# A hybrid decoder step on one core: other orders on GpSimd, VectorE and ScalarE, and a plain fp32 last product

## The chip, the core and the metric

The kernel runs on one core of one Trainium2 chip. The metric is device microseconds (us) of one execution, the median of several runs. A profiled execution gives the trace; its span is the time from the first to the last instruction, a little less than the execution's own time. TensorE is called PE, its weight loads PEld, VectorE DVE, ScalarE ACT, GpSimd POOL and SyncE SP, as in the profile.

## What is computed

One layer of a decoder trunk for 512 prompt tokens and 64 sample tokens (8 sequences of 8), width 1024, all in fp32:

```python
def layer(x, ...):                       # prompt and sample group alike
    h = rmsnorm(x, norm1_g)
    a, b, q, k, v, g = split(h @ w_in)   # 2 x 512 conv columns, 4 x 512 retention columns
    c = silu(layernorm(causal_depthwise_conv(a * sigmoid(b))))        # 31 taps
    o, new_state = retention(rope(q), rope(k), v, state)              # 4 heads, decay per head
    o = silu(g) * groupnorm(o)
    x = x + concat(c, o) @ w_out
    x = x + hier_moe(rmsnorm(x, norm2_g))      # 4 groups x 8 experts, top 2 experts of the top group
    x = x + rmsnorm(p @ w_ple) * sigmoid(x @ w_ple_gate)
    return x, new_conv_buffer, new_state
# hier_moe: hid = silu(t @ w_gate[e]) * (t @ w_up[e]);  y += gate * (hid @ w_down[e]),  32 experts, 256 wide
```

A last RMSNorm ends it. The conv buffers and the retention states of both groups are outputs too.

## The kernel before

The 576 tokens lie in five tiles: 0 to 3 are the prompt's 128 rows each, 4 the 64 sample rows. Each engine has its own program, written out by hand, and they meet at named semaphores: what an engine does next is the order of its own program, and a wait holds up all that stands behind it there.

**Products in three parts.** Most products are made in fp32r, with each operand split in a high part (a rounded copy, mostly by ACT) and a low part (operand less high part, by DVE or POOL). PE adds three products: high by high, then high weight by low operand (`which` 1 in the output projection), then low weight (`which` 2). So a weight chunk `c` needs `w_high(c)` on ACT (L1462) and `w_low(c)` on POOL (L1791) or DVE. A few products are plain fp32 and need no parts: the router, the embedding product with `ple_weights`, and the retention.

**Output projection.** `w_out_part(c, i)` makes chunk `c` (12 to 15, 256 columns each) of tile `i`: 24 matmuls. The order on PE is (12,0), `gated_T(3)`, (12,1) to (12,3), `retention_out(4)`, (13,0) to (13,3), `gated_T(4)`, `sample_states` for heads 0 and 1, (12,4), (13,4), `sample_states` for heads 2 and 3, `p_T`, and then (14,i) and (15,i) by tile with `p_T`, the router and the transposes `h2_T` between them. The first of them waits for `z_sb` 40, ACT's last copy of the input projection (`z_out(11,4)`).

**What feeds it.** `heads_high(i)` (ACT, L1535) and `heads_low(i)` (DVE, L1076) split the retention half of tile `i`; `add_x(c,i)` (DVE, L1071) adds a chunk to the residual. For each tile DVE makes `qTx` (L1091, L1096 for the sample tile), `Sm` (L1103), the group norm's statistics (L1131 to L1136), and, after POOL's power (`grs`, L1859), the normalised output (L1139); POOL then gates it (L1866), which `gated_T(i)` waits for. POOL also makes the key decay (`kz`, L1835), the masked sample queries (`qmask`, L1852, from `qTx`) and value masks for even heads (`v_masks`, L1842); DVE makes those for odd heads (L1082). DVE's L1153 adds to the sample states, which an ACT-queue transfer (`rs_out`) then stores.

**First router norm.** `x1_sq(i)` (ACT, L1584 and L1587) makes the sum of squares and the root, `norm2(i)` (DVE, L1171 and L1176) the normalised tile, `h2_T(i)` on PE the transpose. `norm2(0)` waits for `rs_out`, since it writes where the states lie. `pT_out(n, ...)` (ACT, L1612) copies the transposes that `p_T` makes.

**Experts.** 32 experts, each one step: PE does `gate_up` (48 matmuls), the next expert's `x_T`, the former expert's `down` and `hid_T`. ACT copies high parts (`x_out` L1658, `w_high_part` L1607, `hid_high` L1682, `down_high` L1689) and the result (`y_copy` L1677); DVE makes low parts (`x_low` L1296, `w_low` L1165, `hid_low` L1310, `down_low` L1317). POOL gathers token rows and scatters results. Weights come in a ring of six 1 MB slots, loaded by SP as they are freed. After the last scatter the results are read back and the embedding gate follows.

Of the kernel before, what the change touches and what calls it, by code (L numbers as in the profile page):

```python
# [28 lines left out]
P = 128  # L29
# [95 lines left out]
def build(nc, ins, outs):  # L125
# [8 lines left out]
    with ExitStack() as ctx:  # L134
# [272 lines left out]
        def _(sp):  # L407
# [75 lines left out]
            with sp.If(n_ov > 0):  # L483
                sp.wait_ge(S["d_done"], NE)
# [16 lines left out]
        def _(pe):  # L501
# [356 lines left out]

            def down(i, q):
# [37 lines left out]
            down(LOOPS - 1, NX - 1)  # L897
# [63 lines left out]
        def _(dve):  # L961
# [123 lines left out]
            for i in range(TT):  # L1085
# [8 lines left out]
                else:  # L1094
                    for h in range(NH):
                        m = V.tensor_tensor(qTx[:, h, 0:NS].rearrange("p (b t) -> p b t", b=NB),  # L1096
                                            qTs[:, h, 0:NS].rearrange("p (b t) -> p b t", b=NB),
                                            bc(C("xi")[:, h * P:h * P + NL], 1, NB), ALU.mult)
                        if h == NH - 1:
                            m.then_inc(S["qTx_sb"], 1)  # L1100
# [16 lines left out]
                if i == TT - 1:  # L1117
                    for t in range(TT - 1):
                        heads_low(t)
                    for t in range(TT - 1):  # L1120
                        add_x(12, t)
# [14 lines left out]
                V.tensor_scalar(mv[0:r, :, 1], mv[0:r, :, 1], EPS, None, ALU.add).then_inc(S["gn_var"], 1)  # L1136
                dve.wait_ge(S["gn_rstd"], i + 1)
# [6 lines left out]
            for n in range(2 * NH):  # L1144
                h, a = n // 2, n % 2
                if n == 4:
                    heads_low(TT - 1)
                    add_x(12, TT - 1)
                    add_x(13, TT - 1)
                    v_masks(3)  # L1150
# [169 lines left out]
            def step(i, q, first=False, last=False):  # L1320
# [6 lines left out]
                hid_low(i, q)  # L1327
                down_low(i, q)

            w_low(0, 0, 1)  # L1330
            x_low(0, 0)
# [113 lines left out]
        def _(act):  # L1445
# [126 lines left out]
            heads_high(TT - 1)  # L1572
            w_high(14)
# [80 lines left out]
            def x_out(i, q):  # L1654
                i, par = 2 * i + q // 2, q % 2
                act.wait_ge(S["xt_ps"], 2 * i + par + 1)
                for a in range(2):
# [8 lines left out]
            def y_copy(i, q):  # L1666
                i, par = 2 * i + q // 2, q % 2
                act.wait_ge(S["d_done"], 2 * i + par + 1)
# [7 lines left out]
                for a in range(2):  # L1676
                    A.activation(yout[:, par, a * 512:(a + 1) * 512], bank[5 + a][:, :], ACT.Copy).then_inc(S["y_ready"], 1)  # L1677

# [12 lines left out]
            def step(i, q, first=False, last=False):  # L1691
# [7 lines left out]
                hid_high(i, q)  # L1699
# [287 lines left out]
```

## Time and profile before

| | us |
|---|---|
| runs | 782.49, 783.19, 784.65 (median 783.19) |
| the profiled execution, its own time | 783.66 |
| its span | 781.6 |
| PE busy | 705.3 |
| DVE busy | 556.6 |
| ACT busy | 398.2 |
| POOL busy | 325.9 |

What lies outside the span is 2.06 us. In timeline rows the first number is the start from the span's begin, the second the time taken, and a bracket at the end tells how long the engine had been idle and what ended that. PEclk is the clock granted to TensorE as a share of 2.4 GHz: 1.00 is 2.4 GHz, 0.50 is 1.2 GHz, and a value between is a stretch with both.

### The profile page before, as it was taken

The page shows a single profiled execution, that of the slowest core. Times are in us where ns is not written, and L with a number is a line of the kernel's source. Part 1 is how long each engine was busy: PE and PEld are TensorE (multiplying, and loading weights), DVE is VectorE, ACT ScalarE, POOL GpSimd, SP SyncE. Part 2 cuts the span into 40 slices and gives each one's busy share as a digit, 9 for nine tenths or more (in the row PEclk, how much of TensorE's full clock was granted, in tenths as well). Part 3 has the DMA queues.
Part 4 walks back from the last instruction along what each step waited for, and adds up shares of the span by engine and source line. Part 5 has one row for each costly group of instructions (what it writes and reads, how often), then busy time and mean ns, then how long its engine had stood idle before and what let it go on. Part 6 is the DMA issues. An engine that isn't in the chain of part 4 may idle for free.

```text
span 781.6 us, 13739 instructions
## 1 busy us (share of the span) xinstructions
PE 705.3 (90%) x5152; PEld 657.4 (84%) x5152; DVE 556.6 (71%) x801; ACT 398.2 (51%) x514; POOL 325.9 (42%) x230
## 2 busy tenths in 40 slices
PE   2979999999988987996899999999999999937995
PEld 1879999998978857963888999999999999827994
DVE  4579999804664262355798888888888888847653
ACT  4321332235440022154678888888888888642221
POOL 3222479971455130002256666666666664110000
PEclk9899999999998988999899999999999999977998
DMA  9631331130037234170588999999999999566211
GB/s 283 196 90 55 109 102 62 55 108 11 2 122 245 68 121 149 56 282 15 180 306 321 344 337 340 348 348 366 380 380 375 366 363 359 206 207 212 60 50 41
DMA packets 54301, 156.67 MB, mean 200 GB/s; under 512 B 8825, under 2 KB 34617, under 8 KB 41129
## 3 DMA queue, kind: packets, MB, share of 16 engines
q1 hardware_dynamic: 38516, 134.03, 47.6%
q10 hardware_dynamic: 9597, 12.58, 5.2%
q0 software_dynamic: 6144, 9.45, 3.5%
q8 instruction: 30, 0.49, 0.2%
q14 instruction: 14, 0.11, 0.0%
HBM read 150.34 MB, written 17.59 MB: 215 GB/s over the span
## 4 chain that ended last, share of the span: by engine, by line
PE 71%; DVE 10%; issue 6%; ACT 4%; DMA 4%; POOL 3%; ACTq 1%; POOLq 0%; DVEq 0%
PE bank L503 65%; PE bank L507 6%; DVE ring_parts L1165 3%; DMA ring<-in_w_expert_up 1%; POOL ring_parts L1791 1%; ACT down_high L1689 1%; DMA gbc<-in_norm_g 1%; DVE hT_high L1296 1%; DVE scratch L986 1%; DVE qTx L1096 1%; DVE z L1139 1%; ACT front L1677 1%; POOL z L1866 1%; DMA uext<-expert_rows 1%; DVE ring_parts L1317 1%
## 5 line engine op out<-in xcount | busy, mean ns | idle before, releaser
L503 PE MATMUL bank<-ring_parts,hT_high 128*128 128x256 f32 (+1 forms) x1552 | 216.8, 285 | 0.0
L503 PEld LDWEIGHTS bank<-ring_parts,hT_high 128*128 128x128 f32 (+1 forms) x1552 | 198.5, 186 | 0.1
L503 PE MATMUL bank<-catT_parts,hT_high 128*128 128x256 f32 x1064 | 148.8, 287 | 5.8 <-DVE hT_high L1296 3.3
L1165 DVE TENSOR_TENSOR ring_parts<-ring,catT_parts 128x2048 fp32r<-128x2048 f32 x64 | 146.4, 2288 | 5.0 <-ACT catT_parts L1607 4.9
L503 PEld LDWEIGHTS bank<-catT_parts,hT_high 128*128 128x128 f32 x1064 | 134.3, 191 | 8.2 <-DVE hT_high L1296 4.6
L1607 ACT ACTIVATE catT_parts<-ring 128x2048 fp32r<-128x2048 f32 x64 | 122.6, 1915 | 22.2 <-PE bank L503 19.1
L1791 POOL TENSOR_TENSOR ring_parts<-ring,ring_parts 128x2048 fp32r<-128x2048 f32 x15 | 69.0, 4602 | 69.5 <-ACT ring_parts L1462 69.1
L1317 DVE TENSOR_TENSOR ring_parts<-ring,down_high 128x2048 fp32r<-128x2048 f32 x32 | 73.4, 2293 | 29.4 <-ACT down_high L1689 29.4
L1043 DVE SCALAR_TENSOR_TENSOR bank<-uext,cpar,bank 128x512 f32<-128x512 f32 x116 | 87.9, 757 | 0.0
L1913 POOL DMA_INDIRECT expert_rows<-front,cur_code x32 | 33.9, 1059 | 96.5 <-issue 88.1
L503 PE MATMUL bank<-down_high,cv_parts 128*128 128x512 f32 x256 | 68.9, 412 | 3.1 <-ACT down_high L1689 3.1
L1689 ACT ACTIVATE down_high<-ring 128x2048 fp32r<-128x2048 f32 x32 | 61.7, 1927 | 0.0
L1506 ACT ACTIVATE z<-bank 128x256 f32<-128x256 f32 (+1 forms) x40 | 15.4, 384 | 82.3 <-PE bank L503 82.3
L503 PEld LDWEIGHTS bank<-down_high,cv_parts 128*128 128x128 f32 x256 | 46.6, 192 | 12.2 <-issue 3.2
L1882 POOL COPY cur_tok<-tokidx 128x1 int32 (+1 forms) x28 | 52.6, 1880 | 0.0
L1677 ACT ACTIVATE front<-bank 128x512 f32<-128x512 f32 x64 | 34.8, 596 | 33.1 <-PE bank L503 33.1
L1882 POOL COPY cur_code<-codes 128x1 int32 (+1 forms) x32 | 47.9, 1497 | 0.2
L1462 ACT ACTIVATE ring_parts<-ring 128x2048 fp32r<-128x2048 f32 x15 | 28.6, 1907 | 35.6 <-PE bank L503 35.6
L1296 DVE TENSOR_TENSOR hT_high<-bank,hT_high 128x512 fp32r<-128x512 f32 x64 | 40.9, 679 | 6.6 <-ACT hT_high L1658 6.6
L507 PE MATMUL bank<-const,scratch 128*128 128x128 f32 (+1 forms) x176 | 26.7, 302 | 20.6 <-DVE scratch L986 15.4
L503 PE MATMUL bank<-hT_high,ring_parts 128*128 128x256 f32 (+1 forms) x256 | 39.7, 307 | 5.4 <-ACT catT L1500 4.1
L503 PE MATMUL bank<-ring_parts,hT_low 128*128 128x256 f32 (+1 forms) x320 | 44.5, 282 | 0.0
(250 smaller groups left out, 1113.2 us busy)
## 6 DMA issues: line engine op xcount, KB each, us to landing
ring<-in_w_expert_gate SPq DMA_DIRECT2D x32, 1024.0 KB
ring<-in_w_expert_up SPq DMA_DIRECT2D x32, 1024.0 KB
ring<-in_w_expert_down SPq DMA_DIRECT2D x32, 1024.0 KB, 7.3
ring<-in_w_in SPq DMA_DIRECT2D x12, 1024.0 KB, 5.3
ring<-in_w_out SPq DMA_DIRECT2D x4, 1024.0 KB, 4.9
ring<-in_w_ple_gate SPq DMA_DIRECT2D x4, 1024.0 KB, 6.5
catT<-in_x_prompt SPq DMA_DIRECT2D x4, 512.0 KB, 8.2
z<-in_x_prompt SPq DMA_DIRECT2D x4, 512.0 KB, 6.0
```

The lines of the kernel that those rows point to most:

```text
L503: return nc.tensor.matmul(out, lhsT, rhs, start=start, stop=stop, skip_group_check=True)
L507: return nc.tensor.transpose(out, in_, ident[0:k, 0:k])
L1043: V.scalar_tensor_tensor(out, uext[:, c, t:t + SEQ], tap, bank[7][:, :], ALU.mult, ALU.add).then_inc(S["convp"], 1)
L1165: V.tensor_tensor(ring_r[:, 3 * par + m, :], ring[:, 3 * par + m, :], cat_r[:, m * CHUNK:(m + 1) * CHUNK].bitcast(F32), ALU.subtract).then ...
L1296: m = V.tensor_tensor(XT_lo[:, par, 4 * a:4 * a + 4, :], bank[2 + a][:, :].rearrange("p (k s) -> p k s", k=4), XT_hi[:, par, 4 * a:4 * a + ...
L1317: V.tensor_tensor(ring_r[:, 3 * par + 2, :], ring[:, 3 * par + 2, :], down_hi[:, :].bitcast(F32), ALU.subtract).then_inc(S["dn_lo"], 1)
L1607: A.activation(cat_r[:, m * CHUNK:(m + 1) * CHUNK], ring[:, s, :], ACT.Copy).then_inc(S["w_hi"], 1)
L1677: A.activation(yout[:, par, a * 512:(a + 1) * 512], bank[5 + a][:, :], ACT.Copy).then_inc(S["y_ready"], 1)
L1689: A.activation(down_hi[:, :], ring[:, 3 * par + 2, :], ACT.Copy).then_inc(S["dn_hi"], 1)
L1791: G.tensor_tensor(ring_r[:, c % 4, :], ring[:, c % 4, :], ring_r[:, 4 + c % 2, :].bitcast(F32), ALU.subtract).then_inc(S["w_lo"], 1)
L1882: G.tensor_copy(dst, src[:, bass.ds(n, 1)]).then_inc(done, 1)
L1913: G.indirect_dma_start(moe_d, bass.IndirectOffsetOnAxis(ap=cur_code[0:r, par:par + 1], axis=0), yout[0:r, par, :], None, bounds_check=2 * ...
```

## The change

In the tile loop of the retention, GpSimd's `w_low(12)` comes ahead of its wait for the statistics of tile 3 and no longer behind the power; ACT's `heads_high(0)` comes ahead of `z_out(11,4)`, `heads_high(1)` ahead of `w_high(13)`; DVE's `heads_low(0)` comes into tile 3, ahead of the wait for the power; the sample tile's `qTx` is one instruction for the four heads. DVE's `v_masks(3)` comes ahead of two `add_x`. ACT gets a dummy root ahead of `w_high(14)` and a dummy silu ahead of the first expert; the third `pT_out` goes behind the first router sum of squares; the second half of the first expert's `x_out` goes to DVE. The last expert's down product is plain fp32: four products in place of twelve, without the parts of the weights and of the hidden rows, its two halves signalled and copied apart. The signal count that SP waits for in the overflow branch rises by one with it.

```diff
@@ PE, last expert (NE = 32)
+            def down_plain(i, q):
+                i, par = 2 * i + q // 2, q % 2
+                pe.wait_ge(S["hT_ev"], 2 * (2 * i + par) + 1)
+                pe.wait_ge(slot_in[3 * par + 2], 16 * i + 16 * (LOADS[3 * par + 2] + 1))
+                pe.wait_ge(S["y_ready"], 2 * (2 * i + par))
+                for a in range(2):
+                    for k in range(2):
+                        m = mm(bank[5 + a][:, :], hidT[:, par, k, :], slot2(3 * par + 2)[:, k, a * 512:(a + 1) * 512],
+                               k == 0, k == 1)
+                    m.then_inc(S["d_done"], 1)
-            down(LOOPS - 1, NX - 1)
+            down_plain(LOOPS - 1, NX - 1)
@@ DVE, tile loop
-                    for h in range(NH):
-                        m = V.tensor_tensor(qTx[:, h, 0:NS].rearrange("p (b t) -> p b t", b=NB),
...
+                    V.tensor_tensor(qTx[:, :, 0:NS].rearrange("p h (b t) -> p h b t", b=NB),
+                                    qTs[:, :, 0:NS].rearrange("p h (b t) -> p h b t", b=NB),
+                                    bc(C("xi").rearrange("p (h t) -> p h t", h=NH)[:, :, 0:NL], 2, NB),
+                                    ALU.mult).then_inc(S["qTx_sb"], 1)
...
-                    for t in range(TT - 1):
+                    for t in range(1, TT - 1):
                         heads_low(t)
...
                 V.tensor_scalar(mv[0:r, :, 1], mv[0:r, :, 1], EPS, None, ALU.add).then_inc(S["gn_var"], 1)
+                if i == TT - 2:
+                    heads_low(0)
                 dve.wait_ge(S["gn_rstd"], i + 1)
@@ DVE, sample states
                     heads_low(TT - 1)
+                    v_masks(3)
                     add_x(12, TT - 1)
                     add_x(13, TT - 1)
-                    v_masks(3)
@@ DVE, experts
-                hid_low(i, q)
-                down_low(i, q)
+                    hid_low(i, q)
+                    down_low(i, q)
             w_low(0, 0, 1)
+            dve.wait_ge(S["xt_ps"], 1)
+            V.tensor_copy(XT_hi[:, 0, 4:8, :], bank[3][:, :].rearrange("p (k s) -> p k s", k=4)).then_inc(S["xt_sb"], 1)
             x_low(0, 0)
@@ ACT, tile loop
+                if i == TT - 1:
+                    heads_high(0)
                 z_out(11, i)
...
                 if i == TT - 1:
-                    heads_high(0)
+                    heads_high(1)
                     w_high(13)
-                    heads_high(1)
                     heads_high(2)
...
             heads_high(TT - 1)
+            A.activation(rst4[:, 0:1], epsb[:, :], ACT.Sqrt)
             w_high(14)
@@ ACT, first router norm
-            pT_out(3, (4,))
             for i in range(TT):
+                if i == 1:
+                    pT_out(3, (4,))
                 if i >= 2:
                     h2_out_low(i - 2)
@@ ACT, experts
+            A.activation(rst4[:, 0:1], epsb[:, :], ACT.Silu)
-            x_out(0, 0)
+            x_out(0, 0, first=True)                 # the first half only
...
+                if last:
+                    hid_plain(i, q)                 # one plain copy of the hidden rows
+                else:
+                    hid_high(i, q)
+                    down_high(i, q)
...
-            y_copy(LOOPS - 1, NX - 1)
+            y_copy(LOOPS - 1, NX - 1, last=True)    # waits for each half by itself
@@ POOL, tile loop
+                if i == TT - 2:
+                    w_low(12)
                 pool.wait_ge(S["gn_var"], i + 1)
                 G.tensor_tensor(grs[0:r, :], mv[0:r, :, 1], half[0:r, 0:NH], ALU.pow).then_inc(S["gn_rstd"], 1)
-                if i == TT - 2:
-                    w_low(12)
```

## Rows read from the trace of the kernel before

**Rows 1.** Busy time by stretch: PE, PEld, DVE, ACT, POOL; PEclk, DMA share, GB/s.

```profile
259.00:271.00 12.00, 12.00 (x100) 11.70 (x100) 3.95 (x16) 0.00 (x0) 2.28 (x2) 1.00 0.35 111
293.00:294.00 1.00, 1.00 (x8) 1.00 (x8) 0.26 (x1) 0.00 (x0) 0.00 (x0) 0.64 0.98 226
313.00:315.00 2.00, 2.00 (x14) 2.00 (x14) 0.35 (x1) 0.00 (x0) 0.00 (x0) 0.70 0.40 160
361.00:363.60 2.60, 2.54 (x18) 0.86 (x15) 1.72 (x7) 1.17 (x4) 0.00 (x0) 1.00 0.00 0
433.00:643.00 210.00, 210.00 (x1527) 198.32 (x1526) 186.34 (x153) 177.26 (x196) 131.90 (x87) 1.00 0.97 358
689.40:691.00 1.60, 1.56 (x4) 1.30 (x5) 1.60 (x1) 0.00 (x0) 0.05 (x1) 0.58 1.10 377
```

**Rows 2.** The timeline from 222 to 251 us, all engines.

```profile
222.67 1.90 ACT L1462 ACTIVATE ring_parts<-ring 128x2048 fp32r<-128x2048 f32 x1
...
228.43 4.55 POOL L1791 TENSOR_TENSOR ring_parts<-ring,ring_parts 128x2048 fp32r<-128x2048 f32 x1
...
229.31 0.62 ACT L1535 ACTIVATE hT_high<-catT 128x512 fp32r<-128x512 f32 x1
...
229.60 0.76 SPq L432 DMA_DIRECT2D front<-in_state_ret  x1
...
229.77 5.78 DVE L1096 TENSOR_TENSOR qTx<-qTs,const 128x64 f32<-128x64 f32 x4
...
233.94 1.26 POOL L1866 TENSOR_TENSOR z<-z 128x512 f32<-128x512 f32 x1
...
235.81 1.88 DVE L1076 TENSOR_TENSOR catT_parts<-catT,hT_high 128x512 fp32r<-128x512 f32 x3
...
236.53 2.07 PE L503 MATMUL bank<-ring_parts,catT_parts 128*128 128x256 f32 x8 [5.28 <-DVE catT_parts L1076]
...
240.11 1.06 PE L507 MATMUL bank<-const,z 128*128 128x128 f32 x4
...
250.30 1.96 PE L503 MATMUL bank<-front,uext 128*64 128x128 f32 x16
...
250.48 0.42 DVE L1071 TENSOR_TENSOR z<-bank,z 128x256 f32<-128x256 f32 x1 [1.51 <-PE bank L503]
```

**Rows 3.** The timeline: one mask alone at 209 us, then 280 to 292 us.

```profile
209.88 1.72 DVE L1082 TENSOR_TENSOR cv<-z,const 64x1024 f32<-64x1024 f32 x1
...
280.39 4.52 POOL L1791 TENSOR_TENSOR ring_parts<-ring,ring_parts 128x2048 fp32r<-128x2048 f32 x1 [5.29 <-ACT ring_parts L1462]
...
281.48 4.51 DVE L1082 TENSOR_TENSOR cv<-z,const 64x1024 f32<-64x1024 f32 x1
...
286.73 3.60 PE L503 MATMUL bank<-cv,kz 64*128 64x512 f32 x4 [3.72 <-DVE front L1153]
...
291.05 1.20 PE L503 MATMUL bank<-ring_parts,conv_high 128*128 128x256 f32 x4
```

**Rows 4.** The timeline at the first router norm.

```profile
304.94 1.05 ACT L1584 ACTIVATE front<-z 128x1024 f32<-128x1024 f32 x1
...
309.26 1.97 PE L507 MATMUL bank<-const,front 128*128 128x128 f32 x8 [4.53 <-DVE front L1176]
```

**Rows 5.** DMA issues: engine queue, count, KB, median us from issue to landing.

```profile
out<-front ACTq DMA_DIRECT2D x1, 2048.0 KB, 10.2
front<-in_state_ret SPq DMA_DIRECT2D x1, 0.5 KB, 13.2
```

**Rows 6.** The timeline: a plain fp32 product, a short gap at 360, the last expert.

```profile
337.42 3.60 PE L503 MATMUL bank<-ple_weights,uext 128*128 128x512 f32 x8
...
360.83 0.84 PE L503 MATMUL bank<-one_hots 128*128 128x80 bf16 x10 [1.32 <-DVE one_hots L1267]
...
689.44 3.56 PE L503 MATMUL bank<-down_high,cv_parts 128*128 128x512 f32 x8 [3.06 <-ACT down_high L1689]
694.06 1.09 ACT L1677 ACTIVATE front<-bank 128x512 f32<-128x512 f32 x2 [4.72 <-PE bank L503]
```

More of the change, by code:

```diff
@@ L483, in _ @@
             with sp.If(n_ov > 0):
-                sp.wait_ge(S["d_done"], NE)
+                sp.wait_ge(S["d_done"], NE + 1)
                 with sp.Fori(0, NOV) as j:
@@ L1094, in _ @@
                 else:
-                    for h in range(NH):
-                        m = V.tensor_tensor(qTx[:, h, 0:NS].rearrange("p (b t) -> p b t", b=NB),
[L1097 to L1100, printed above, removed]
+                    V.tensor_tensor(qTx[:, :, 0:NS].rearrange("p h (b t) -> p h b t", b=NB),
+                                    qTs[:, :, 0:NS].rearrange("p h (b t) -> p h b t", b=NB),
+                                    bc(C("xi").rearrange("p (h t) -> p h t", h=NH)[:, :, 0:NL], 2, NB),
+                                    ALU.mult).then_inc(S["qTx_sb"], 1)
                     decay = C("decay_s", NS).rearrange("p (h t) -> p h t", h=NH)
@@ L1652, in xt_half, with x_out @@
                 return XT[:, par, 0:4, :], bank[2][:, :].rearrange("p (k s) -> p k s", k=4)
-            def x_out(i, q):
+            def x_out(i, q, first=False):
                 i, par = 2 * i + q // 2, q % 2
                 act.wait_ge(S["xt_ps"], 2 * i + par + 1)
-                for a in range(2):
+                for a in range(1 if first else 2):
                     A.activation(XT_hi[:, par, 4 * a:4 * a + 4, :], bank[2 + a][:, :].rearrange("p (k s) -> p k s", k=4),
@@ L1664, in silu, with y_copy @@
                 A.activation(gat[:, par, :], bank[0][:, 0:FF], ACT.Silu).then_inc(S["sil_done"], 1)
-            def y_copy(i, q):
+            def y_copy(i, q, last=False):
                 i, par = 2 * i + q // 2, q % 2
-                act.wait_ge(S["d_done"], 2 * i + par + 1)
+                if not last:
+                    act.wait_ge(S["d_done"], 2 * i + par + 1)
                 if isinstance(i, int):
@@ L1676, in y_copy, with hid_plain @@
                 for a in range(2):
+                    if last:
+                        act.wait_ge(S["d_done"], NE + a)
                     A.activation(yout[:, par, a * 512:(a + 1) * 512], bank[5 + a][:, :], ACT.Copy).then_inc(S["y_ready"], 1)
+            def hid_plain(i, q):
+                i, par = 2 * i + q // 2, q % 2
+                act.wait_ge(S["hT_ps"], 2 * i + par + 1)
+                A.activation(hidT[:, par, :, :], bank[4][:, 0:2 * P].rearrange("p (k s) -> p k s", k=2),
+                             ACT.Copy).then_inc(S["hT_ev"], 1)
             def hid_high(i, q):
@@ L1698, in step @@
                     y_copy(*before(i, q))
-                hid_high(i, q)
-                down_high(i, q)
-            x_out(0, 0)
+                if last:
+                    hid_plain(i, q)
[4 more added lines that the diff above has]
+            x_out(0, 0, first=True)
             step(0, 0, first=True)
```

## The prediction

> **What bounds the kernel now.** The page's busy times come first: PE is busy 705.3 us of a span of 781.6, so the kernel is PE's own work, and time is lost only where PE stands still, or runs at the lower clock after it stood. Then the busy time by stretch. The expert stage is PE without a gap, 210.00 us of 210 [rows 1], and the change touches nothing inside it. What is left is the stretch between the output projection and the first expert, and the end of the last expert. There the timeline shows four places where PE waits for another engine: 5.28 us for DVE's low part of tile 0 [rows 2], 3.72 us for DVE's last value mask [rows 3], 4.53 us for the first router norm [rows 4], and 3.06 us for the high part of the last down weights [rows 6]. After each of them the matmuls ran at half clock for some us: the granted clock is 0.64 in 293 to 294, 0.70 in 313 to 315 and 0.58 in 689.4 to 691, while the dense stretch from 259 shows 1.00 with 100 matmuls in 12 us, 2.9 us for a tile of 24 [rows 1].
>
> **The change part by part.** All times are on the axis of the profiled execution before.
>
> *First wait, retention to output projection.* DVE's four `qTx` instructions take 5.78 us for 64 elements a row each, while three `heads_low` of 512 elements take 1.88 [rows 2]. The reason stands beside them: POOL runs `w_low(12)` from 228.43 to 232.98 and further work to 235.20, and a DVE instruction with two inputs in SBUF gets through only between POOL's instructions. Only then comes `heads_low(0)`, and PE goes on at 236.53.
> After the change `w_low(12)` starts when `w_high(12)` ends, at 224.6 (222.67 + 1.90), and ends at 229.2. The power for tile 3, queued behind it on POOL (before, right ahead of it), comes at 229.2 and takes about 1 us. On DVE the normalisation of tile 3 is queued behind `heads_low(0)`, which waits for `heads_high(0)`: that one ended at 229.93 and hardly moves (it changes place with a copy of 0.4 us). So `heads_low(0)` ends between 230.3 (no meeting with POOL) and 230.9 (blocked by the power until 230.2, then 0.63). PE, which stood from 231.25 (236.53 - 5.28), needs it then: no stall.
> The next wait is `gated_T(3)`, which stands right behind (12,0) in PE's order. Its chain: normalisation of tile 3 until 231.8 to 232.3, then POOL's gating, 1.26 us [rows 2] or up to 0.4 more beside DVE: 233.1 to 234.0. (12,0) has 16 matmuls left at 231.25 and ends at 233.0, so PE stands 0.1 to 1.0 us. `gated_T(3)` then starts at 233.2 to 234.1 instead of 240.11, takes 0.5, and three tiles of 2.86 us follow: `retention_out(4)` at 242.3 to 243.2 instead of 250.30. Next in line there: the sample states, issued at 229.6 [rows 2] and landing after 13.2 us [rows 5], at 242.8; and POOL's masked queries, four instructions of 512 elements, by its gating of that size 5.0 us, or 6.9 if DVE's 1.88 comes between, from 234 on: 241 at the latest. The single `qTx` costs 0.4 to 0.9 (256 elements; four times the shortest part), off PE's path by then. I take 243.1: **7.2 us saved**. Behind `retention_out(4)` (9.0 us) PE needs the residual adds of column 12 at 252; in the trace of before the last of them came at 250.48 and waited for PE, not for its transfer [rows 2], so nothing stands there.
> The Trainium skill bears on this (SBUF — State Buffer, Who interferes with whom): a DVE instruction with two SBUF inputs and a GpSimd instruction that reads SBUF exclude each other for the whole instruction. The trace agrees, with 5.78 us. The same section says that `tensor_scalar` can take the shared ports too. `w_low(12)` now lies over such an instruction of tile 3's statistics, and no run here shows the two together. By that rule the statistics end at 229.4 and not 227.4, and the sum loses 0.2 us, since the power waits for `w_low(12)` anyhow.
>
> *Second wait, sample states.* `v_masks(3)` takes 1.72 us alone and 4.51 beside POOL's `w_low(14)` [rows 3]; it was queued behind two adds that wait for (12,4) and (13,4), and PE stood from 283.01 to 286.73. Ahead of them it has two tiles and two products of 1 us, 7.8 us of PE's work, before PE needs it: it starts near 283.0 - 7.8 - 7.2 = 268.0 and is over by 270 to 271, while POOL is idle from 267.9 (280.39 - 5.29 - 7.2) to `w_low(14)` at 273.2. The adds behind it wait for PE's tiles until 271 anyhow. PE goes from the fourth head pair to the last without a gap: two products of about 1 us and `p_T` of 0.6 take 2.5 us where 283.01 to 291.05 was 8.0, 5.5 saved. (14,0) then ran at half clock until 293.7 (0.64 in 293 to 294), 2.7 us that shrink by 1.2. **6.7 us.** Late next: DVE's state adds, about 0.7 us for 512 elements each; they end within each 1 us product.
>
> *Third wait, first router norm.* ACT stood in `pT_out(3)` until PE had done (15,1); only then came the sum of squares at 304.94, a table load, the root, `norm2(0)` on DVE, and PE's transposes at 309.26. After the change the sum of squares follows the second `pT_out`, right after (15,0), some 6 us earlier against PE. PE loses neither the 4.53 us nor the half clock up to 314.2 (0.70 in 313 to 315), which costs the transposes 1.0 (1.97 for 8) and (14,2) 1.1. **6.6 us.** Late next is `norm2(0)`'s wait for `rs_out`: PE's last state product ends at 277.9 (283.0 + 2.1 - 7.2), the add at 278.6, the 2 MB store goes out at 279.0 behind another issue, lands after 10.2 us [rows 5] at 289.2, and the norm of 1024 elements takes 1.25, by `heads_low`'s 0.63 for 512: 290.5. PE is there at 304.73 - 13.9 = 290.8. So it just fits, and each us more of that store is a us more of time. Behind the later `pT_out(3)` on ACT stand one store and the next sum of squares, which wait for DVE until then anyhow. The dummy root puts the table load into ACT's wait for (12,4), 2.9 us of PE work; uncovered it would cost at most the 3.3 us from 306.0 to 309.26 [rows 4].
>
> *First expert.* `x_out` is two copies of 128 by 512 from PSUM on ACT, 1.09 us as in the last expert [rows 6]; with the second on DVE, idle there, PE starts about **0.4 us** earlier. The dummy silu moves a table load from beside PE's first product to an idle time: nothing.
>
> *Last expert.* PE ended its own work at 686.38; the copies for the expert before and the hidden rows end at 687.54 (689.44 less the 1.9 of `down_high`), and PE may start at 687.6. Four plain fp32 products are 8 instructions, 3.60 us at full clock [rows 6]: the first half is done at 689.4, the second at 691.2, its copy of 0.6 at 691.9. Before, the copies ended at 695.15. **3.3 us**, and all that follows (scatter, read back, the gate weights' parts) hangs on those copies. At half clock the 8 take 7.2 and the copy ends at 695.4, 0.2 later than before. DVE and ACT lose work there that nobody waits for. The raised count in SP's overflow branch costs nothing: it falls on the same instant.
>
> Sum: 7.2 + 6.7 + 6.6 + 0.4 + 3.3 = 24.2, less about 0.5 for a signal at each of the five joints: 23.7. Against the profiled execution of 783.66 (span 781.6 and 2.06 around it) that is 760.0; the median of the runs is 0.47 lower, which gives **759.5**.
>
> **The rivals.**
> (a) *The clock falls in the gaps that remain*, 0.1 to 1.0 us before `gated_T(3)` and 1.2 us in the last expert. For it: the clock fell after gaps of 3 to 5 us. Against: after a gap of 1.32 us that ended at 360.83 [rows 6] the clock in 361 to 363.6 is 1.00 [rows 1]. Price: 5 us at half clock in the first, 2.5, and all of the last expert's 3.3 and 0.2 more: 765.5.
> (b) *The store takes the place of the third wait.* It shares the DMA engines with two expert weights that now start closer to it. At the 13.2 us of the load of the same states it is 3 us late: 762.5. For it: there is no slack; against: the loads of 1 MB should have ended by 280.
> (c) *POOL and DVE meet more than I count*, because `heads_low(0)` or the new `qTx` falls between POOL's key decay and gating: up to 2 more instructions of about 1 us each on the way to `gated_T(3)`: 761.5.
> (d) *Slower: the expert stage's transfers.* In 433 to 643 the DMA share is 0.97 at 358 GB/s [rows 1]; 1527 matmul instructions at 70 a step are 21.8 steps of 9.63 us, 3.45 MB each. PE has no gap there, so the two run neck and neck. If the earlier start changed how gathers and loads fall together and the rate sank, every step would wait. It decides at 23.7 + 2.35 us over 32 steps, 0.81 a step, that is below 330 GB/s; at 316 GB/s it would be 10.9 us a step and 800 us in all. Against it: every load is started by PE's own progress, so the stage should shift as a whole; a share of 0.97 leaves it a small chance. The Trainium skill (SBUF — State Buffer, Summary: rules for kernel authors) gives about 358 GB/s for HBM to SBUF; the trace agrees to the figure, and by that rule the stage has no slack.
> (e) *No change*: PE's waits are only handed on, to the sample states at 242.8 and the store, if both are several us later than in the trace.
>
> **How the numbers follow.** Forecast 0.72 (757.5 to 761), (a) 0.09, (b) and (c) together 0.12, (d) 0.03, (e) 0.02, and 0.02 for more than I see. The forecast's own ends come from the bounds above: 0.9 less or more at the first wait, 0.5 at the joints, 1 us of the store. The range takes in (b), (c) and (a): 756.5 to 766. A measurement of this kernel tells about 0.3%, 2.35 us, from no change. Faster by more: 0.72 + 0.09 + 0.12 + 0.02 = 0.95; within: 0.02; slower: 0.03.
>
> **What would show it.** Right: `retention_out(4)` near 243, `h2_T(0)` near 291 with PE at clock 1.00 from 230 on, the first expert's product near 351, and 691.9 - 686.4 = 5.5 us from PE's last transposes to the last copy. Wrong: a PE wait of several us before `gated_T(3)` (c), a wait of `norm2(0)` for a transfer (b), clock 0.50 in the last expert (a), or steps above 9.7 us (d). I would be most wrong if the lock between DVE and POOL also held for the small statistics and pushed the gating behind 236.

## The result, and the profile after

The kernel after takes 759.9 us (median; 759.27, 759.39, 760.41 and 763.2) beside 783.4 us for the kernel before in the same comparison: a ratio of 0.970, 95% interval 0.966 to 0.973, so 21.1 to 26.3 us less. 759.5 was predicted, in a range of 756.5 to 766. Four executions in the comparisons of this document took far longer than the others of their kernel (820.68 and 2404.15 us of the kernel before, 987.35 of a1, 1274.78 of c2) and enter no ratio and no range.

The profiled execution of the kernel after took 760.41 us, its span 758.4. From its page of the profile, the busy times and each engine's share of the chain of work that ended last:

```profile
PE 698.0 (92%) x5148; PEld 650.0 (86%) x5148; DVE 547.1 (72%) x797; ACT 396.5 (52%) x514; POOL 325.4 (43%) x230
...
PE 73%; DVE 9%; DMA 6%; issue 4%; ACT 4%; POOL 2%; ACTq 1%; SPq 0%; POOLq 0%; DVEq 0%
```

PE's busy time falls by 7.3 us only. Most of the 23.2 us of the span is time in which PE stood; the rest is mostly time in which the same matmuls ran at half clock. Both show in the timeline. At the first wait (start, time taken, engine, line, operation, tiles; the bracket is the idle time before it and what ended it):

```profile
224.78 4.57 POOL L1820 TENSOR_TENSOR ring_parts<-ring,ring_parts 128x2048 fp32r<-128x2048 f32 x1 [3.53 <-ACT ring_parts L1475]
227.33 2.05 DVE L1145 TENSOR_SCALAR mv<-mv 128x4 f32<-128x4 f32 x1
229.16 0.63 ACT L1548 ACTIVATE hT_high<-catT 128x512 fp32r<-128x512 f32 x1 [2.22 <-PE bank L503]
229.46 1.01 POOL L1890 TENSOR_TENSOR grs<-mv,half 128x4 f32<-128x4 f32 x1
229.83 0.69 DVE L1087 TENSOR_TENSOR catT_parts<-catT,hT_high 128x512 fp32r<-128x512 f32 x1 [0.45 <-ACT hT_high L1548]
231.79 0.42 DVE L1106 TENSOR_TENSOR qTx<-qTs,const 128x256 f32<-128x256 f32 x1
231.96 1.41 POOL L1895 TENSOR_TENSOR z<-z 128x512 f32<-128x512 f32 x1 [0.48 <-DVE z L1150]
232.46 4.44 DVE L1087 TENSOR_TENSOR catT_parts<-catT,hT_high 128x512 fp32r<-128x512 f32 x3
233.42 0.66 PE L507 MATMUL bank<-const,z 128*128 128x128 f32 x4 [0.20 <-POOL z L1895]
242.91 1.93 PE L503 MATMUL bank<-front,uext 128*64 128x128 f32 x16 [0.30 <-DMA front<-in_state_ret]
```

`w_low(12)` now starts at 224.78 instead of 228.43, and `heads_low(0)` takes 0.69 us and is done at 230.5, before PE asks for it. PE's wait of 5.28 us [rows 2] is 0.20 us ahead of `gated_T(3)`, which starts at 233.42 instead of 240.11. `retention_out(4)` starts at 242.91 and waits 0.30 us for the sample states. The three later `heads_low` now meet POOL (4.44 us for three, 1.88 before) and nobody waits for them.

At the second and the third wait:

```profile
268.65 1.21 DVE L1093 TENSOR_TENSOR cv<-z,const 64x1024 f32<-64x1024 f32 x1
275.57 1.95 PE L503 MATMUL bank<-cv,kz 64*128 64x512 f32 x4
278.69 0.45 ACTq L1592 DMA_DIRECT2D out<-front  x1
284.96 1.06 ACT L1599 ACTIVATE front<-z 128x1024 f32<-128x1024 f32 x1
289.41 1.28 DVE L1187 SCALAR_TENSOR_TENSOR front<-z,rst,gbc 128x1024 f32<-128x1024 f32 x1 [2.79 <-DMA out<-front]
290.75 1.16 PE L507 MATMUL bank<-const,front 128*128 128x128 f32 x8 [0.31 <-DVE front L1187]
```

The mask takes 1.21 us with POOL idle (4.51 in [rows 3]; the 1.72 us there, which the prediction took for a mask alone, were beside POOL's gating from 208.84 to 210.51) and is over 5.7 us before PE reads it; the 3.72 us wait is gone. The square starts at 284.96 instead of 304.94 [rows 4], and DVE's norm now waits 2.79 us for the store of the states, which ends when PE is about done with the tile before: PE stands 0.31 us, not 4.53.

At the last expert, PE's plain products and ACT's two copies:

```profile
667.85 3.70 PE L503 MATMUL bank<-ring,cv 128*128 128x512 f32 x8 [1.22 <-ACT cv L1701]
669.93 0.60 ACT L1696 ACTIVATE front<-bank 128x512 f32<-128x512 f32 x1 [2.13 <-PE bank L503]
671.58 0.60 ACT L1696 ACTIVATE front<-bank 128x512 f32<-128x512 f32 x1 [1.06 <-PE bank L503]
```

From PE's last hidden transposes (666.62) to the end of the last copy (672.18) it is 5.6 us, 8.8 before.

How the gain builds up, for all kernels: positions in the two traces, and below them the gain in us against the kernel before. So that the scatter at the start of an execution (up to 3 us) doesn't enter, the gains are counted from the start of (12,0); "end" is the span's, and the last digit is uncertain by one.

| | `retention_out(4)` | `h2_T(0)` | first router product | first `gate_up` | first `down` | last `hid_T`, end | `x2_T(0)` | end |
|---|---|---|---|---|---|---|---|---|
| before, at us | 250.30 | 309.26 | 315.29 | 371.87 | 389.74 | 686.37 | 706.66 | 781.6 |
| after, at us | 242.91 | 290.75 | 294.59 | 350.52 | 369.70 | 666.62 | 683.89 | 758.4 |
| after | 7.4 | 18.6 | 20.7 | 21.4 | 20.1 | 19.8 | 22.8 | 23.2 |
| a1_tail_only | 1.2 | 0.2 | -0.3 | -0.3 | -1.4 | -0.5 | 2.6 | 2.5 |
| a2_first_wait_only | 7.8 | 7.0 | 6.7 | 6.7 | 5.7 | 4.9 | 4.1 | 3.5 |
| a3_mask_only | 1.2 | 8.1 | 8.7 | 8.3 | 6.3 | 7.1 | 7.2 | 6.6 |
| a4_norm_only | 0.2 | 4.8 | 7.0 | 7.0 | 7.1 | 8.0 | 8.0 | 7.7 |
| b1_pool_order_back | 4.3 | 15.4 | 17.6 | 17.8 | 16.3 | 16.4 | 19.6 | 19.6 |
| b2_low_back | 2.7 | 13.4 | 15.6 | 15.3 | 13.4 | 13.0 | 16.1 | 16.2 |
| b3_four_queries | 7.6 | 18.3 | 20.5 | 20.8 | 19.2 | 19.7 | 22.8 | 22.7 |
| b4_store_late | 7.8 | 15.0 | 16.0 | 15.6 | 13.9 | 14.1 | 17.2 | 17.2 |
| b5_x_out_whole | 7.8 | 18.9 | 21.1 | 20.9 | 19.9 | 20.2 | 23.3 | 23.6 |
| b6_no_table_first | 7.5 | 18.6 | 20.8 | 21.0 | 19.3 | 18.6 | 21.8 | 22.0 |
| c1_warm_first | 7.6 | 18.7 | 20.9 | 22.2 | 23.9 | 24.3 | 27.4 | 26.7 |
| c2_warm_both | 7.4 | 18.9 | 21.1 | 22.5 | 24.2 | 23.7 | 26.8 | 27.9 |

The three waits give 20.7 us by the first router product. 1.6 us are lost between the first `gate_up` and the last hidden transposes, and 3.0 come back at the last expert. The row of a1 is the scale for reading the others: nothing is moved there ahead of the last expert, and still its columns differ from the kernel before by up to 1.4 us.

### The profile page after: what moved, and what is told of

It is laid out like the page before. It is cut to its first block, busy times and chain, and to the rows that moved or that the text cites. A ratio compares the mean times of both kernels' runs of the same rounds, so it can differ in the third digit from the quotient of the medians.

```text
span 758.4 us, 13727 instructions
## 1 busy us (share of the span) xinstructions
PE 698.0 (92%) x5148; PEld 650.0 (86%) x5148; DVE 547.1 (72%) x797; ACT 396.5 (52%) x514; POOL 325.4 (43%) x230
## 4 chain that ended last, share of the span: by engine, by line
PE 73%; DVE 9%; DMA 6%; issue 4%; ACT 4%; POOL 2%; ACTq 1%; SPq 0%; POOLq 0%; DVEq 0%
PE bank L503 67%; PE bank L507 6%; DVE ring_parts L1176 2%; DMA front<-in_state_ret 2%; DMA out<-front 1%; DMA catT<-in_x_prompt 1%; DMA ring<-in_w_expert_up 1%; POOL ring_parts L1820 1%; DVE ring_parts L1417 1%; ACT down_high L1714 1%; DVE hT_high L1307 1%; DVE ring_parts L1328 1%; ACT front L1696 1%; DVE scratch L997 1%; DMA scratch<-h_rows,tokidx 1%
## 5 line engine op out<-in xcount | busy, mean ns | idle before, releaser
L1622 ACT ACTIVATE catT_parts<-ring 128x2048 fp32r<-128x2048 f32 x64 | 122.6, 1916 | 22.4 <-PE bank L503 19.9
L1328 DVE TENSOR_TENSOR ring_parts<-ring,down_high 128x2048 fp32r<-128x2048 f32 x31 | 71.1, 2292 | 27.9 <-ACT down_high L1714 27.9
L1054 DVE SCALAR_TENSOR_TENSOR bank<-uext,cpar,bank 128x512 f32<-128x512 f32 x116 | 86.1, 742 | 0.0
L503 PE MATMUL bank<-down_high,cv_parts 128*128 128x512 f32 x248 | 65.3, 405 | 0.0
L1714 ACT ACTIVATE down_high<-ring 128x2048 fp32r<-128x2048 f32 x31 | 59.7, 1927 | 0.0
L1519 ACT ACTIVATE z<-bank 128x256 f32<-128x256 f32 (+1 forms) x40 | 15.3, 383 | 80.1 <-PE bank L503 80.1
L503 PEld LDWEIGHTS bank<-down_high,cv_parts 128*128 128x128 f32 x248 | 44.3, 189 | 8.4
L507 PE MATMUL bank<-const,scratch 128*128 128x128 f32 (+1 forms) x176 | 26.7, 303 | 20.5 <-DVE scratch L997 15.6
L507 PEld LDWEIGHTS bank<-const,scratch 128*128 128x128 f32 (+1 forms) x176 | 23.9, 199 | 22.7 <-issue 15.2
```

What stands on the lines that cost most here:

```text
L503: return nc.tensor.matmul(out, lhsT, rhs, start=start, stop=stop, skip_group_check=True)
L507: return nc.tensor.transpose(out, in_, ident[0:k, 0:k])
L1054: V.scalar_tensor_tensor(out, uext[:, c, t:t + SEQ], tap, bank[7][:, :], ALU.mult, ALU.add).then_inc(S["convp"], 1)
L1328: V.tensor_tensor(ring_r[:, 3 * par + 2, :], ring[:, 3 * par + 2, :], down_hi[:, :].bitcast(F32), ALU.subtract).then_inc(S["dn_lo"], 1)
L1622: A.activation(cat_r[:, m * CHUNK:(m + 1) * CHUNK], ring[:, s, :], ACT.Copy).then_inc(S["w_hi"], 1)
L1714: A.activation(down_hi[:, :], ring[:, 3 * par + 2, :], ACT.Copy).then_inc(S["dn_hi"], 1)
```

## The experiments

Ratios are to the kernel before, measured on the same chip, with 95% intervals; the gain in us is worked out with 784 us.

**The four parts alone.** Each adds one part of the change to the kernel before.

```diff
 a1: the last expert's down_plain, hid_plain and split y_copy, as in the change
 a2: POOL: w_low(12) ahead of the power; ACT: heads_high(0), (1) earlier;
     DVE: heads_low(0) in tile 3, one qTx instruction
 a3  @@ DVE, n == 4
+    v_masks(3)
     add_x(12, TT - 1)
     add_x(13, TT - 1)
-    v_masks(3)
 a4  @@ ACT
-pT_out(3, (4,))
 for i in range(TT):
+    if i == 1:
+        pT_out(3, (4,))
```

> The kernel before with the last expert's plain fp32 down product alone, nothing moved elsewhere. Theory: from the end of PE's last hidden transposes to the end of the last output copy it takes about 5.5 us where the kernel before took 8.8 (686.38 to 695.15), at granted clock 1.00 in the products, and everything behind the copies moves by the same: about 3.2 us off the whole time, 780.2 beside 783.4. Rival (a) of the prediction, the clock falls in the gap of about 1.2 us ahead of the products: the eight instructions take about 7.2 us, the copies end about where they did, and the time changes by 0.2 us at most. If all five gains are independent this run and the next three add up to the 23.5 us of the whole change; if they are handed on from one wait to the next, their sum is another.

> The kernel before with the edits around the sample queries alone (POOL's low part of column 12 ahead of the power, the high and low part of tile 0 earlier, one sample query instruction); mask, router norm and last expert as before. Theory: the 5.28 us stall ahead of the output projection's tile 0 goes, gated_T(3) starts near 233.4 and retention_out(4) near 243, 7.4 us earlier, and the waits for the mask and for the router norm stay as they are, 3.7 and 4.5 us: 776 us. Rival (waits are handed on): the sample states, which land near 242.8, or the mask, which is set off by DVE's adds, take the gain back in part: less than 5 us off the whole time, with longer stalls ahead of the state products.

> The kernel before with the last sample mask alone moved ahead of the two residual adds on DVE. Theory: PE's stall of 3.72 us for the mask goes, and with it the 1.8 us of half clock behind it: 6.7 us off the whole time, 776.7, with router norm's 4.5 us stall unchanged behind it. Rival: PE's stall is only moved to the adds of DVE that now come later, or POOL's low parts of columns 14 and 15 become late: under 4 us.

> The kernel before with the third p_T copy alone moved behind the first router norm's square on ACT, without the dummy root. Theory: the square comes 6 us earlier, the table load of the root is hidden, and PE loses neither the 4.53 us stall nor the half clock behind it: about 6.6 us off, 776.8. The 2 MB store of the states, which norm2(0) waits for, is 13.9 us earlier against the axis than it may be late here, so it should land before (about 301.7 against 303 needed). Rival (b): the store takes the stall's place; then norm2(0) waits for a transfer and the gain is 3 us or less.

| | ratio | gain, us | predicted for the part |
|---|---|---|---|
| a1 | 0.9975 (0.9959 to 0.9991) | 2.0 (0.7 to 3.2) | 3.3 |
| a2 | 0.9920 (0.9894 to 0.9946) | 6.3 (4.2 to 8.3) | 7.2 |
| a3 | 0.9913 (0.9880 to 0.9947) | 6.8 (4.2 to 9.4) | 6.7 |
| a4 | 0.9911 (0.9885 to 0.9938) | 7.0 (4.8 to 9.0) | 6.6 |

The four sum to 22.1 us, the whole change gives 23.7 by its ratio: the parts add up within their intervals. That no wait was handed on to another is shown by the traces, place by place. In a2 the first wait is gone and the other two stand as they were, now in PE's rows at 278.72 and 302.02:

```profile
233.17 0.65 PE L507 MATMUL bank<-const,z 128*128 128x128 f32 x4 [0.20 <-POOL z L1867]
278.72 3.75 PE L503 MATMUL bank<-cv,kz 64*128 64x512 f32 x4 [3.75 <-DVE front L1153]
302.02 1.97 PE L507 MATMUL bank<-const,front 128*128 128x128 f32 x8 [4.53 <-DVE front L1176]
```

Those are 3.72 and 4.53 us in [rows 3, 4]. In a3 and a4 it is the one wait that the edit is for that is gone, and the others stand as they were (5.26 and 4.53 us in a3, 5.28 and 3.74 in a4). a1's last expert is that of the kernel after, to 0.01 us at most (eight matmul instructions of 3.70 us behind a gap of 1.23), and gives 3.1 us from the last `hid_T` to `x2_T(0)` (from -0.5 to 2.6 in the table). Its whole time shows 2.0 (0.7 to 3.2), so the 3.1 lie at the edge of what the runs allow. In its trace the first experts took 1.1 us longer than in the trace of before, though nothing had been moved ahead of them; a2's trace, too, loses 1.1 us there, and in other places that its edit leaves alone, so that it ends only 3.5 us ahead where its runs say 6.3. The section on why comes back to that. Rival (a) in the last expert is out: at half clock the eight would have taken 7.2 us.

**What in the first wait carries the gain.** From the kernel after, one order at a time is put back.

```diff
 b1  @@ POOL, tile 3
-if i == TT - 2:
-    w_low(12)
 G.tensor_tensor(grs[0:r, :], mv[0:r, :, 1], half[0:r, 0:NH], ALU.pow)...
+if i == TT - 2:
+    w_low(12)
 b2  @@ DVE
-for t in range(1, TT - 1):           # tile 4
+for t in range(TT - 1):
     heads_low(t)
-if i == TT - 2:                      # tile 3, ahead of the wait for the power
-    heads_low(0)
 b3  @@ DVE, sample tile: four qTx instructions of 64 elements, as before
```

> The kernel after with POOL's low part of column 12 put back behind the power of tile 3. Theory of the prediction: POOL's power would come early, but the low part then lies over the sample queries and the low part of tile 0, so DVE is blocked until about 233: the chain to gated_T(3) ends about 3 us later, retention_out(4) near 246, and the whole time is 2 to 4 us above the kernel after, since the store that norm2(0) waits for moves with it. Rival: DVE's place in the order alone (the low part of tile 0 ahead of the normalisation) carries the gain, and POOL's order is worth under 0.5 us.

> The kernel after with the low part of tile 0 put back into tile 4 on DVE, behind the sample queries. Theory: PE stands again ahead of the output projection's tile 0 until the single query instruction and POOL's work let it pass: about 2.4 us later at retention_out(4) than in the kernel after, and about as much at the end. Rival: the single query instruction and POOL's new order carry the gain alone: within 0.5 us of the kernel after.

> The kernel after with four sample query instructions on DVE again instead of one. Theory of the prediction: they lie off PE's path now, so at most 1 us at retention_out(4), and between 0 and 1 us at the end. Rival: the lock between DVE and POOL stretches the four as it did before (5.8 us), the masked values come late, and retention_out(4) or the state products lose 3 us or more.

b1 measured 0.9768 (0.9748 to 0.9788), b2 0.9762 (0.9738 to 0.9786), b3 0.9722 (0.9692 to 0.9752), beside 0.9698 for the kernel after. In b1, where POOL's low part starts at 228.88 again, the trace reads:

```profile
227.65 0.17 DVE L1145 TENSOR_SCALAR mv<-mv 128x4 f32<-128x4 f32 x1
228.88 4.55 POOL L1820 TENSOR_TENSOR ring_parts<-ring,ring_parts 128x2048 fp32r<-128x2048 f32 x1
230.15 3.83 DVE L1087 TENSOR_TENSOR catT_parts<-catT,hT_high 128x512 fp32r<-128x512 f32 x1 [2.33 <-ACT hT_high L1548]
234.03 2.08 PE L503 MATMUL bank<-ring_parts,catT_parts 128*128 128x256 f32 x8 [2.38 <-DVE catT_parts L1087]
```

`heads_low(0)` takes 3.83 us where the kernel after has 0.69: DVE's instruction with two SBUF inputs gets through when POOL's 4.55 us are over, at 233.4. The row is one of its own for the lock that the prediction argued from four stretched `qTx`. `retention_out(4)` is 3.1 us later than in the kernel after, as the theory had it. The end is 3.7 us later by the traces, within the expected 2 to 4, and 5.5 by the ratios, whose intervals are too wide to tell the two apart. In b2 `heads_low(0)` goes behind the normalisation and the sample queries and PE waits 2.60 us for it:

```profile
233.91 2.08 PE L503 MATMUL bank<-ring_parts,catT_parts 128*128 128x256 f32 x8 [2.60 <-DVE catT_parts L1087]
235.79 1.05 PE L503 MATMUL bank<-ring_parts,conv_high 128*128 128x256 f32 x4
240.86 0.64 PE L503 MATMUL bank<-ring_parts,conv_high 128*128 128x256 f32 x4
```

The loss at `retention_out(4)` is 4.7 us (at the end 7.0 by the traces, 5.0 by the ratios), twice the expected 2.4: the expectation counted the gap alone. Four matmuls that take 0.64 us take 1.05 until nearly 240, and that is most of the other half. So neither order is enough without the other (4.3 us are left in b1 and 2.7 in b2, of 7.4): in the kernel after they meet so that DVE's low part falls into POOL's 1.0 us of power and not into its 4.6 us of subtraction. ACT's new order was not put back alone; in the trace it can be worth little there, since `heads_high(0)` ends at 229.79 after and at 229.93 before [rows 2]. b3's four queries cost nothing that shows at `retention_out(4)` (0.2 us earlier than in the kernel after, where the half clock doesn't play in) and 0.2 us at `h2_T(0)`; its ratio can't be told from that of the kernel after. So with the other orders in place the single query instruction adds nothing that these rows show.

**How close the store is.** In b4 ACT issues the store of the states behind the second `pT_out`.

```diff
 @@ ACT
-act.dma_start(ret_s[0].rearrange("b h d e -> d b h e"), states).then_inc(S["rs_out"], 16)
 ...
 pT_out(2, (2, 3))
+act.dma_start(ret_s[0].rearrange("b h d e -> d b h e"), states).then_inc(S["rs_out"], 16)
```

> The kernel after with the store of the sample states issued later on ACT, behind the second p_T copy, about 6.4 us later. It measures rival (b)'s price. Theory of the prediction, no slack: each us that the store lands later is a us more of time, so norm2(0) ends about 6 us later, PE stands that long, and some 2 us of half clock come behind it: 6 to 8 us above the kernel after. Rival: the store has several us of slack, since norm2(0) waits for the square and the root anyhow, or a store alone on the queue lands faster: 0 to 3 us.

0.9779 (0.9755 to 0.9803): by the ratios 6.3 us more than the kernel after, by the traces 6.0. The store's issue, the norm and the transposes in the timeline, and the store's row in the list of DMA issues (last the us from issue to landing):

```profile
284.06 0.40 ACTq L1643 DMA_DIRECT2D out<-front  x1
292.90 1.29 DVE L1187 SCALAR_TENSOR_TENSOR front<-z,rst,gbc 128x1024 f32<-128x1024 f32 x1 [6.63 <-DMA out<-front]
294.24 1.97 PE L507 MATMUL bank<-const,front 128*128 128x128 f32 x8 [4.16 <-DVE front L1187]
```

```profile
out<-front ACTq DMA_DIRECT2D x1, 2048.0 KB, 8.7
```

The issue is 5.4 us later, but the transfer takes 8.7 us and not the 10.6 of the kernel after, so the norm starts 3.5 us later and `h2_T(0)` as much. Then the clock adds its part: the transposes take 1.97 instead of 1.16, and at the first router product the loss is 4.7. The prediction's "each us more of that store is a us more of time" holds for the landing up to `h2_T(0)`, and the half clock behind a new gap comes on top: a landing 3.5 us later cost 6.0 at the end. The stretch that this puts at risk is real: the kernel after already waits for that transfer.

**The two small edits.** Put back one at a time: both copies of the first `x_out` on ACT (b5), and no dummy root (b6).

```diff
 b5  -x_out(0, 0, first=True)   +x_out(0, 0)       (and DVE's copy goes)
 b6  -A.activation(rst4[:, 0:1], epsb[:, :], ACT.Sqrt)
```

> The kernel after with both copies of the first expert's input on ACT again. Prediction: 0.4 us above the kernel after. Rival, from the trace of the kernel after: the first expert runs at granted clock 0.50 for about 4 us whichever copy is early, and PE waits for that clock and for the weights of the next step: within 0.2 us of it.

> The kernel after without the dummy root ahead, so that the table load lies behind the first square again. Theory: norm2(0) waits for the store until 289.41, and square, load and root would end near 287.7: 0 us. Rival: the load lies on the chain to norm2(0), and with the root and the reciprocal behind it the time grows by its 1.3 us.

b5: 0.9719 (0.9689 to 0.9750); b6: 0.9705 (0.9678 to 0.9733). Neither can be told from the kernel after by its time. In b5's trace it takes 3.12 us from the first expert's transposes to its first `gate_up`, as in the kernel before, and 2.72 in the kernel after: the split does what was predicted. At the first `down` b5 is only 0.2 us behind the kernel after, so half of it is given back by then, and the rest is less than what the table scatters by. The dummy silu was not tried alone. In b6 the table load is back behind the square, and DVE still waits for the store after it:

```profile
287.35 1.28 ACT L1601 ACT_TABLE_LOAD   x1
288.65 0.29 ACT L1601 ACTIVATE rst<-ssq,epsb 128x1 f32<-128x1 f32 x1
290.68 1.28 DVE L1187 SCALAR_TENSOR_TENSOR front<-z,rst,gbc 128x1024 f32<-128x1024 f32 x1 [1.54 <-DMA out<-front]
```

The load takes 1.28 us and 1.54 us of DVE's wait are left over. b6's last columns, 1.2 us below those of the kernel after, arise in the first experts, as in a1.

**The clock of the first expert.** The dummy products multiply constants into a bank that nothing reads.

```diff
 @@ PE
+def warm(n):
+    for _ in range(n):
+        mm(bank[7][:, :], ident, C("decay"), True, True)
+warm(5)                              # c1 and c2: ahead of the first expert's x_T
 ...
 down_plain(LOOPS - 1, NX - 1)
+warm(12)                             # c2 alone
```

> The kernel after with five dummy plain fp32 products on PE ahead of the first expert's transposes, of constants, into a bank that nothing reads: more work than needed. Theory (the clock carries it): PE stands there waiting for the first expert's input, its clock is 0.50 for about 4 us afterwards, and filled with products it would be 1.00: the first gate and up products take half of their time, about 3 us off the kernel after, 757. Rival: the wait for the input, not the clock, sets the next steps (transfers of weights or gathered rows set the pace): 0, and if the products delay the transposes, up to 2 us slower.

> The kernel before it (five dummy products ahead of the first expert) with twelve more of them on PE behind the last expert's down product, where PE waits for the rows to be scattered and read back, also of constants and read by nothing. Theory: the clock that the overflow and gate stage starts with is then 1.00 and not 0.50: a further 2 to 3 us off, about 754.5, some 5.5 below the kernel after. Rival: that stage's start is paced by the transfers and by DVE's and ACT's weight parts, so no further gain; or the products outlast the wait and it is 1 us slower.

c1 took 758.6 us (757.83 to 759.67), ratio 0.9671 (0.9649 to 0.9693); c2 756.7 (755.27 to 758.73), ratio 0.9652 (0.9627 to 0.9678). Beside them on the same chip b5 and b6, which are the kernel after but for one small edit each, lie at 759.8 to 764.0, wholly above both. The kernel after itself was measured in a comparison of its own, and there the intervals overlap (0.9664 to 0.9731 for it). PE's rows in the kernel after, then in c1:

```profile
347.80 1.94 PE L507 MATMUL bank<-const,scratch 128*128 128x128 f32 x8 [4.97 <-DMA scratch<-h_rows,tokidx]
350.52 2.08 PE L503 MATMUL bank<-catT_parts,hT_high 128*128 128x256 f32 x8 [0.78 <-DVE hT_high L1343]
```

```profile
345.31 4.56 PE L503 MATMUL bank<-const 128*128 128x512 f32 x10
350.54 1.13 PE L507 MATMUL bank<-const,scratch 128*128 128x128 f32 x8 [0.67 <-DMA scratch<-h_rows,tokidx]
352.45 1.21 PE L503 MATMUL bank<-catT_parts,hT_high 128*128 128x256 f32 x8 [0.78 <-DVE hT_high L1349]
```

The transposes take 1.13 us and the first eight products 1.21, where the kernel after has 1.94 and 2.08, and the dummies delay nothing, since the gathered rows land behind them: in both kernels the transposes start 117.7 us after (12,0). At the first `down` c1 is 3.8 us ahead of the kernel after, at the last hidden transposes 4.5; the theory had 3. In c2 the first transposes behind the dummies are fast too, and then the clock falls all the same:

```profile
668.45 10.46 PE L503 MATMUL bank<-const 128*128 128x512 f32 x24
680.87 1.16 PE L507 MATMUL bank<-const,z 128*128 128x128 f32 x8 [1.95 <-DVE z L1402]
684.31 1.91 PE L503 MATMUL bank<-ring_parts,hT_high 128*128 128x256 f32 x8
```

The dummies ended 1.95 us before the transposes. c2's stage from `x2_T(0)` to the end takes 73.9 us, the kernel after's 74.5 and c1's 75.7. Of the expected 2 to 3 us c2 gains 0.7 against the first and 1.8 against the second; by the two whole times it is 1.5 (0.9671 less 0.9652), within the intervals. c2 is the fastest kernel here, with a margin over c1 that isn't settled.

## Why the prediction was right

**The first wait**, 7.2 predicted, 7.4 found. All its times were met: `w_low(12)` from 224.8 to 229.35 (224.6 to 229.2 predicted), `heads_low(0)` done at 230.5 (230.3 to 230.9), gating until 233.4 (233.1 to 234.0), `retention_out(4)` at 242.9 (243.1), held there by the transfer that was named as next. Rival (c) is out: of the instructions that it names, `qTx` starts at 231.79, 0.17 us ahead of the gating, and runs beside it; the gating takes 1.41 us, 0.15 more than before. The later bound for `heads_low(0)` stood for a DVE instruction that waits for the whole of POOL's power. That didn't show: it took 0.69 us beside the power's 1.01, and as much in b3. POOL's long subtraction blocks it (b1), the power doesn't. The rule of the Trainium skill (SBUF — State Buffer, Who interferes with whom) that `tensor_scalar` can take the shared ports too is borne out: L1145 takes 2.05 us beside POOL's low part in the kernel after, and 0.17 in b1, where POOL is idle at that time. It cost nothing much, as worked out: the power waited for the same low part, which ended at 229.35.

**The second and third wait**, 6.7 and 6.6 predicted. From `retention_out(4)` to (15,0), at 295.17 before and 280.88 after, 6.9 us were gained; from there to the first router product (315.29 and 294.59) 6.4. The store was issued at 278.69 (279.0 predicted) and landed after 10.6 us; the norm ended at 290.7 (290.5). Rival (b) is there by the sign that the prediction named, a wait of `norm2(0)` for a transfer, 2.79 us of DVE's time, but PE lost only 0.31 us to it and not 3; b4 shows what a later landing would have cost. The clock's fall in the gaps that remain, rival (a), didn't come: the granted clock is 1.00 from 230 to 321 and in the last expert's products.

**The last expert**, 3.3 predicted, 3.2 found up to the last copy (695.15 and 672.18 less the 19.75 of the last hidden transposes). 0.2 us of it are lost to ACT and DVE, which hold `x2` up with their parts of the gate weights until 681.22.

**The expert stage**, rival (d): in the stretch of even steps the rate is the one of before [rows 1].

```profile
414.00:622.60 208.60, 208.60 (x1516) 196.86 (x1515) 184.85 (x153) 176.91 (x195) 130.25 (x87) 1.00 0.96 358
```

From the same product to the same transposes it takes 208.93 us before (433.75 to 642.68) and 209.16 after (413.70 to 622.86).

**Terms that were mis-sized.** The prediction gave the first expert 0.4 us, which were there, and the experts behind it nothing; what stood there was a loss of 1.6 us between the first `gate_up` and the last `hid_T`. With it the sum of what was found reads 7.4 + 6.9 + 6.4 + 0.6 (first router product to first `gate_up`) - 1.6 + 3.2 - 0.2 + 0.5 (the gate stage) = 23.2, against 24.2 less 0.5 of the prediction. That the total is met within 0.5 us is in part luck: the gate stage, which the change doesn't touch either, happened to be 0.5 us shorter, and the 0.5 us taken off for signals at the joints didn't show as a loss of their own. Where most of the 1.6 went can be read in the granted clock. First before, then after, then a1, two or three stretches each of the second step (columns: stretch, us, busy time of PE, PEld, DVE, ACT and POOL with instructions, granted clock, DMA share, GB/s):

```profile
381.87:383.87 2.00, 1.62 (x13) 1.43 (x13) 2.00 (x2) 2.00 (x4) 1.92 (x2) 1.00 0.95 403
383.87:385.87 2.00, 1.61 (x14) 1.41 (x13) 2.00 (x4) 0.62 (x1) 0.00 (x0) 1.00 0.27 90
```

```profile
360.52:362.52 2.00, 1.47 (x8) 1.28 (x9) 2.00 (x2) 2.00 (x5) 1.98 (x2) 0.90 0.99 418
362.52:364.52 2.00, 2.00 (x12) 2.00 (x11) 2.00 (x5) 1.06 (x1) 0.38 (x1) 0.50 0.43 133
364.52:366.52 2.00, 2.00 (x15) 2.00 (x15) 2.00 (x1) 0.29 (x2) 0.00 (x0) 0.75 0.04 8
```

```profile
382.80:384.80 2.00, 1.61 (x8) 1.42 (x9) 2.00 (x1) 2.00 (x4) 1.98 (x2) 0.79 0.96 408
384.80:386.80 2.00, 2.00 (x12) 2.00 (x11) 2.00 (x5) 0.87 (x1) 0.19 (x1) 0.50 0.31 94
```

PE enters that step with the same two gaps in all three, 1.2 us ahead of the hidden transposes and 0.4 behind them. Before, the clock held at 1.00 through them; after and in a1 it fell to 0.50. a1 has the unchanged order up to there, so the fall isn't something that the change does. Over all fourteen kernels the time from the first `gate_up` to the first `down` follows the granted clock of that stretch: 16.2 us at 1.00 (c1 and c2, which enter it at full clock), 17.8 to 17.9 at 0.89 to 0.90 (before and a4), and 18.9 to 19.8 at 0.80 down to 0.76 (the other ten). So the clock carries the difference; what decides between the two kinds in a given execution stays open, with one trace for each kernel. The step of the prediction that failed is its assumption that a stretch which isn't touched costs after what it cost in the one trace of before: that trace was one of the two fast ones, 1.0 to 2.0 us below the other ten.

## What to carry to other kernels

Read a stall of TensorE back to the instruction that came last, and then ask what stood ahead of that instruction in its engine's own program: here changes of order at three places, which took hardly any work away from what TensorE waited for, gave 21 of 23 us. A DVE instruction with two SBUF inputs that TensorE waits for belongs into a place where GpSimd has short instructions or none, and here the orders of both engines had to change for that. Price a stall with the half clock behind it (0.8 to 2.1 us on top of the gap in b1, b2 and b4); where the stall itself has to stay, products that nothing waits for, put into it, gave 2 to 4 us at the first expert (c1's ratio beside those of the kernel after, b5 and b6), and at the end of the last expert nothing that is settled.

## What was not expected of the hardware

When the clock falls in a stall, and so when it is back at full speed, scatters from execution to execution. Behind the same stall of 5.28 us ahead of tile 0, the granted clock of before is 0.50 in 240 to 242 and 0.87 in 242 to 244, while a1, whose stall ended 0.6 us later, has 0.85 and 1.00 in the same stretches. In a1 the clock had fallen earlier in the stall: it is 0.50 in 234 to 236, where before still has 0.92. That is the 1.2 us in a1's first column.

The clock also fell where PE had no gap. In the router, with PE busy for all of each stretch, the kernel after shows:

```profile
323.00:325.00 2.00, 2.00 (x21) 1.48 (x21) 1.88 (x6) 1.91 (x5) 0.00 (x0) 0.89 0.85 352
325.00:327.00 2.00, 2.00 (x4) 0.96 (x3) 1.76 (x9) 1.90 (x4) 0.00 (x0) 0.50 0.24 88
327.00:329.00 2.00, 2.00 (x4) 0.72 (x4) 1.73 (x10) 0.88 (x3) 0.00 (x0) 0.76 0.50 190
```

What PE did before the fall were 32 matmuls of 36 columns (3.03 us, from 321.28). In c1 the same matmuls (from 323.81) are followed by no fall, the granted clock is 1.00 there, so they don't decide it by themselves. It cost nothing here: as said above, the first expert's transposes start 117.7 us after (12,0) with the fall and without. No run was made on what decides it.
